# Conditioning sums by column groups, working values in PSUM, SWA scores and one value pair moved: seven edits to a two-block transformer kernel

## What is computed

```python
cond = silu(c)
for i in range(2):
    mod = cond @ ada_w[i] + ada_b[i]               # 1024 -> 6 * 1024
    sh1, sc1, g1, sh2, sc2, g2 = split(mod, 6)
    h = modulate(rms_norm(x, norm_g[i, 0]), sh1, sc1)
    y = nsa_mixer(h, ...) if i == 0 else swa_sink_mixer(h, ...)
    x = x + (1 + g1) * rms_norm(y, norm_g[i, 1])
    h = modulate(rms_norm(x, norm_g[i, 2]), sh2, sc2)
    y = (relu(h @ w_up) ** 2) @ w_down             # 1024 -> 4096 -> 1024
    x = x + (1 + g2) * rms_norm(y, norm_g[i, 3])
```

## Time and profile before

| what | us |
|---|---|
| device time, median of 3 runs (their range) | 2114.76 (2109.31 to 2120.08) |
| profiled execution, its own time | 2111.6 |
| its span | 2109.8 |
| PE busy | 1987.3 (94%) |
| DVE busy | 1208.1 (57%) |
| POOL busy | 950.7 (45%) |
| ACT busy | 699.0 (33%) |

### The profile page before, as it was taken

The page is one execution under the profiler, slowest core; times in us unless marked ns, Lnnn a source line. Parts: engine busy times, 40 slices in busy tenths (PEclk is TensorE's granted clock), DMA queues, the critical chain, the costliest instruction groups (busy, mean ns, idle before and its releaser), DMA issues.

```text
span 2109.8 us, 26670 instructions
## 1 busy us (share of the span) xinstructions
PE 1987.3 (94%) x10136; PEld 1631.9 (77%) x10136; DVE 1208.1 (57%) x1721; ACT 699.0 (33%) x1217; POOL 950.7 (45%) x552
## 2 busy tenths in 40 slices
PE   6999999889999998888999999899999989999997
PEld 5887777668888886766788888787897678888885
DVE  7576776873745667656623426686463338546163
ACT  3343554321222233553322223342343332222122
POOL 1465554454454445444444444542374134444442
PEclk9999999999999999999999999998999999999998
DMA  7774322435555424622222323221243123323221
GB/s 280 230 215 162 110 91 90 150 140 180 195 173 190 170 71 130 180 81 70 90 91 99 100 90 100 71 79 62 100 140 100 40 70 100 98 91 100 92 99 60
DMA packets 79985, 252.16 MB, mean 120 GB/s; under 512 B 12160, under 2 KB 12672, under 8 KB 79616
## 3 DMA queue, kind: packets, MB, share of 16 engines
q1 hardware_dynamic: 79872, 250.61, 35.9%
HBM read 235.21 MB, written 15.37 MB: 119 GB/s over the span
## 4 chain that ended last, share of the span: by engine, by line
PE 69%; issue 12%; DVE 8%; POOL 8%; ACT 3%; POOLq 0%; DVEq 0%; ACTq 0%
PE ps L885 19%; PE ps L887 18%; PE ps L886 18%; POOL wl L785 5%; PE ps L1128 3%; PE ps L1100 2%; PE ps L1071 2%; DVE rs L1933 2%; DVE st L1785 1%; PE ps L1365 1%; PE ps L1026 1%; POOL pr L806 1%; PE ps L1388 1%; ACT pr L2457 1%; POOL al L835 1%
## 5 line engine op out<-in xcount | busy, mean ns | idle before, releaser
L785 POOL TENSOR_TENSOR wl<-raw,wh 128x1024 fp32r<-128x1024 f32 x309 | 777.7, 2522 | 1001.7 <-ACT wh L2313 1001.7
L2313 ACT CAST wh<-raw 128x1024 fp32r<-128x1024 f32 x309 | 322.3, 1049 | 916.7 <-PE ps L887 838.4
L885 PE MATMUL ps<-ah,wh 128*128 128x512 f32 x1240 | 488.4, 394 | 1.4 <-DVE pair L1715 1.4
L886 PE MATMUL ps<-ah,wl 128*128 128x512 f32 x1240 | 483.2, 390 | 0.0
L887 PE MATMUL ps<-al,wh 128*128 128x512 f32 x1240 | 483.1, 390 | 0.0
L885 PE MATMUL ps<-hh,wh 128*128 128x512 f32 x688 | 272.2, 396 | 14.6 <-DVE hl L1935 10.8
L885 PEld LDWEIGHTS ps<-ah,wh 128*128 128x128 f32 x1240 | 233.3, 188 | 52.8 <-issue 3.2
L887 PE MATMUL ps<-hl,wh 128*128 128x512 f32 x688 | 272.4, 396 | 0.0
L886 PEld LDWEIGHTS ps<-ah,wl 128*128 128x128 f32 x1240 | 233.4, 188 | 49.6 <-issue 1.7
L887 PEld LDWEIGHTS ps<-al,wh 128*128 128x128 f32 x1240 | 233.1, 188 | 48.9
L886 PE MATMUL ps<-hh,wl 128*128 128x512 f32 x688 | 270.5, 393 | 0.0
(11 more groups left out here) (360 smaller groups left out, 2915.0 us busy)
## 6 DMA issues: line engine op xcount, KB each, us to landing
raw<-in_units SPq DMA_DIRECT2D x309, 512.0 KB, 3.5
ada_mlp<-in_ada SPq DMA_DIRECT2D x64, 512.0 KB, 3.3
ada<-in_ada SPq DMA_DIRECT2D x16, 512.0 KB, 16.1
qs<-qscr SPq DMA_DIRECT2D x32, 256.0 KB, 3.4
ada_in<-in_ada SPq DMA_DIRECT2D x16, 512.0 KB, 3.5
ks<-kscr SPq DMA_DIRECT2D x24, 256.0 KB, 4.5
x<-in_xT SPq DMA_DIRECT2D x1, 2048.0 KB, 13.4
qscr<-rot_h SPq DMA_DIRECT2D x16, 128.0 KB, 2.4
```

Source lines behind the costliest of these rows:

```text
L785: nc.gpsimd.tensor_tensor(wl[:, slot], raw[:, slot], wh[:, slot].bitcast(F32), ALU.subtract).then_inc(lo_done, 1)
L885: nc.tensor.matmul(out_ap, wh[:, slot, k], high[:, k0 + k], start=first and k == 0, stop=False)
L886: nc.tensor.matmul(out_ap, wl[:, slot, k], high[:, k0 + k], start=False, stop=False)
L2313: a.copy(wh[:, slot], raw[:, slot]).then_inc(hi_done, 1)
```

## The change

1. The conditioning sums of `ada_late` take ones (128 by 32) as the stationary side and the 128 by 1024 sum as the moving side, 128 columns at a time, and write four groups of 32 partitions; DVE copies the row out (`ada_fold`) and TensorE turns it with two transposes (`ada_turn`). The sites are now: in `nsa_out` the sum after the fifth unit and the turn after the seventh; in `mlp0` the sum after the third unit of a block and the turn after the sixth; the last one after the sixth unit of block 7, with its turn in `swa_in`.
2. In NSA, blocks 2 and 0, which lie side by side in a bank, share one mask product of 256 columns.
3. In the setup the conditioning sums in the making, the scale coefficient's input and the scaled chunks of the first norm are in PSUM.
4. In the MLP the square is made as max(b, 0) times `rs` and written to PSUM bank 5 or 7; ACT and the subtraction read it there.
5. In SWA the first two works' scores, maxima, exponentials and scaling are placed inside `swa_in` (`EARLY`), TensorE's after the eighth of its eleven units; they use banks 4 to 7. The two batches of `turn` change places, with a count of `p_scaled` for each. The last query rotary is no longer split.
6. Two of the value units of the memory are multiplied in the fourth head of the cross-attention (`last_values`), in two halves, where the other heads have query units.
7. Some DVE steps change places (`ada_take(7)` behind a rotary), and a ScalarE copy of the setup is ahead of the root.

```diff
-TURNS = {"nsa": (((0, 0),), ((1, 0), (3, 384)), ((2, 0),)), "swa": (((0, 0), (1, 256)), ((2, 0), (3, 256)))}
-COPIES = {"nsa": (("act", 512), ("dve", 512), ("dve", 256)), "swa": (("dve", 512), ("act", 384))}
+TURNS = {"nsa": (((0, 0),), ((1, 0), (3, 384)), ((2, 0),)), "swa": (((2, 0), (3, 256)), ((0, 0), (1, 256)))}
+COPIES = {"nsa": (("act", 512), ("dve", 512), ("dve", 256)), "swa": (("act", 384), ("dve", 512))}
...
-        return b if self.nsa else 2 * (w % 2) + b
+        if self.nsa:
+            return b
+        return 2 * (w % 2) + b + (4 if w < EARLY else 0)
...
+                        if i == 2:
+                            op.then_inc(p_scaled, 1)
                 op.then_inc(p_scaled, 1)
 
             def centre(w):
...
-                    for part in range(2):
+                    for part in range(1 if plan.nsa and i == 2 else 2):
                         nc.tensor.matmul(o, qs[:, Q_SLOT[j], i * P:(i + 1) * P], ks[:, slot, part, k0 * P:k1 * P],
-                                         start=part == 0, stop=False)
-                    if plan.nsa or i == 0:
+                                         start=part == 0 and not (plan.nsa and i == 0), stop=False)
+                    if plan.nsa and i == 2:
+                        mm = nc.tensor.matmul(o, qs[:, Q_SLOT[j], i * P:(i + 1) * P], ks[:, slot, 1, k0 * P:k1 * P],
+                                              start=False, stop=False)
+                    elif plan.nsa and i == 0:
+                        mm = nc.tensor.matmul(ps[:, bank, col - P:col + P], ident_r[:],
+                                              mask_r[:, 1:2].to_broadcast([P, 2, P]), start=False, stop=True)
+                    elif plan.nsa or i == 0:
                         mm = nc.tensor.matmul(o[:, width - P:width], ident_r[:], mask_r[:, 1], start=False, stop=True)
                     else:
                         mm = nc.tensor.matmul(o, ident_r[:], mask_r[:].rearrange("p a k -> p (a k)"), start=False, stop=True)
...
                 for b, parts in enumerate(plan.turns):
+                    if not plan.nsa:
+                        pe.wait_ge(p_scaled, 2 * n - plan.nth0 + 1 + b)
...
         def ada_late(k):
             pe.wait_ge(adc_used, 8 * (k + 1))
-            ada(ps[:, 6, 8 * k:8 * k + 8], acc_mlp[:, k % 2])
+            for half in range(2):
+                for j in range(4):
+                    m = 4 * half + j
+                    mm = nc.tensor.matmul(ps[32 * j:32 * j + 32, 6, half * P:(half + 1) * P], small("ones")[:, 0:32],
+                                          acc_mlp[:, k % 2, m * P:(m + 1) * P], start=True, stop=True)
+            mm.then_inc(ada_sum, 1)
+        def ada_turn(k):
+            pe.wait_ge(ada_copied, k + 1)
+            for half in range(2):
+                mm = nc.tensor.transpose(ps[:, 6, (2 + half) * P:(3 + half) * P], ada_row[:, half * P:(half + 1) * P],
+                                         small("ident"))
+            mm.then_inc(ada_sum, 1)
...
+                        gemm(u, 3, ah, al)
+                    if late:
+                        ada_late(b)
+                    gemm(u + 3, 3, ah, al)
+                    if late:
+                        ada_turn(b)
+                    gemm(u + 6, 2, ah, al)
...
         attention(PLAN_NSA)
-        gemm_squared(FIRST["nsa_out"], ah, al, ready=(o_split, 0), midway=lambda: ada_late(0), adds=True)
+        gemm_squared(FIRST["nsa_out"], ah, al, ready=(o_split, 0), adds=True,
+                     between=lambda c: ada_late(0) if c == 4 else ada_turn(0) if c == 6 else None)
         mlp("mlp0", 0)
         gemm_first(FIRST["swa_in"], ah, al, A_READY["swa_in"])
-        gemm(FIRST["swa_in"] + 3, UNITS_SWA_IN - 3, ah, al)
+        gemm(FIRST["swa_in"] + 3, 1, ah, al)
+        ada_turn(7)
+        gemm(FIRST["swa_in"] + 4, 4, ah, al)
+        attention(PLAN_SWA, early=True)
+        gemm(FIRST["swa_in"] + 8, UNITS_SWA_IN - 8, ah, al)
+        assert done[0] % RING == 3
         attention(PLAN_SWA)
...
+        def last_values(i):
+            assert LAST_VALUES % RING == 3
+            n, t = done[0], slice(i * P, (i + 1) * P)
+            if i == 0:
+                pe.wait_ge(lo_done, LAST_VALUES + 2)
+                bank_free(n)
+            o = ps[:, n % RING, i * 256:i * 256 + 256].rearrange("p (a f) -> p a f", a=2)
+            for k in range(DC):
+                nc.tensor.matmul(o, mh[:, k, t], wh[:, 0:4:3, k], start=k == 0, stop=False)
+                nc.tensor.matmul(o, mh[:, k, t], wl[:, 0:4:3, k], start=False, stop=False)
+                mm = nc.tensor.matmul(o, ml[:, k, t], wh[:, 0:4:3, k], start=False, stop=k == DC - 1)
+            if i:
+                mm.then_inc(unit_used, 2)
+                done[0] += 1
         xscores(0, 0)
         for h in range(4):
             if h < 3:
                 gemm(XQ0 + 2 * h + 2, 1, ah, al)
+            else:
+                last_values(0)
             xturn(h, 0)
             xscores(h, 1)
             if h < 3:
                 gemm(XQ0 + 2 * h + 3, 1, ah, al)
+            else:
+                last_values(1)
             xturn(h, 1)
             if h < 3:
...
             def scaled(c):
-                v.scalar_tensor_tensor(out=tt[:, c % 3], in0=src_t[:, c], scalar=gain(c), in1=inv,
...
                 dve.wait_ge(high_made, n0 + c + 1)
-                t, h = tt[:, c % 3], high[:, c].bitcast(F32)
...
 
+        def so_far(i):
+            return ps[:, 2 * i:2 * i + 2].rearrange("p b s -> p (b s)")
         dve.wait_ge(cond_done, 1)
         for k in range(8):
             dve.wait_ge(ada_in[k], 16)
             if k == 0:
-                op = v.tensor_scalar(acc0[:], ada0[:, k], cond[:, 0:1], None, ALU.mult)
+                op = v.tensor_scalar(so_far(0), ada0[:, k], cond[:, 0:1], None, ALU.mult)
             else:
-                op = v.scalar_tensor_tensor(out=acc0[:], in0=ada0[:, k], scalar=cond[:, k:k + 1], in1=acc0[:],
-                                            op0=ALU.mult, op1=ALU.add)
+                op = v.scalar_tensor_tensor(out=acc0[:] if k == 7 else so_far(0), in0=ada0[:, k], scalar=cond[:, k:k + 1],
+                                            in1=so_far(0), op0=ALU.mult, op1=ALU.add)
             op.then_inc(ada_first, 1)
...
                 w = ada0[:, 12 + i]
                 if i == 0:
-                    op = v.tensor_scalar(acc1[:], w, cond[:, 4:5], None, ALU.mult)
+                    op = v.tensor_scalar(so_far(1), w, cond[:, 4:5], None, ALU.mult)
                 else:
-                    op = v.scalar_tensor_tensor(out=acc1[:], in0=w, scalar=cond[:, 4 + i:5 + i], in1=acc1[:],
-                                                op0=ALU.mult, op1=ALU.add)
+                    op = v.scalar_tensor_tensor(out=acc1[:] if i == 3 else so_far(1), in0=w, scalar=cond[:, 4 + i:5 + i],
+                                                in1=so_far(1), op0=ALU.mult, op1=ALU.add)
                 op.then_inc(scale_part_made, 1)
                 dve.wait_ge(scale_part_made, i + 1)
...
-        ada_read_out(1, ps[:, 7, 0:8])
-        ada_coef(0, 0)
-        norm("nsa_in", x, coef_at(0, 0), coef_at(0, 1), ah, al, root=False, after=first_shift)
+        link(v.tensor_tensor(ps[:, 7, 8:16], ps[:, 7, 0:8], small("ada_b")[:, 8:16], ALU.add))
+        link(v.scalar_tensor_tensor(out=coef[:, 0, 0], in0=ps[:, 7, 8:16], scalar=1.0, in1=small("norm_g")[:, 0:8],
+                                    op0=ALU.add, op1=ALU.mult))
+        norm("nsa_in", x, coef_at(0, 0), coef_at(0, 1), ah, al, root=False, after=first_shift, place=first_place)
 
 
...
         def ada_take(k):
 
-            dve.wait_ge(ada_sum, 4 + k)
-            ada_read_out(4 + k, ps[:, 6, 8 * k:8 * k + 8])
+            dve.wait_ge(ada_sum, 2 * k + 5)
+            turned = ps[:, 6, 2 * P:4 * P].rearrange("p (a f) -> p a f", a=2)[:, :, 0:P:32]
+            at0 = 8 * (4 + k)
+            link(v.tensor_tensor(mod[:, at0:at0 + 8].rearrange("p (a f) -> p a f", a=2), turned,
+                                 small("ada_b")[:, at0:at0 + 8].rearrange("p (a f) -> p a f", a=2), ALU.add))
+        def ada_fold(k):
+            dve.wait_ge(ada_sum, 2 * k + 4)
+            v.tensor_copy(ada_row, ps[:, 6, 0:2 * P]).then_inc(ada_copied, 1)
 
         def mlp(layer):
...
                     k = hid[0]
-                    t = rs[:, k % 2]
-                    v.tensor_scalar(t, bank(), 0.0, None, ALU.max).then_inc(evac, 1)
-                    dve.wait_ge(evac, banks[0])
-                    v.tensor_tensor(t, t, t, ALU.mult).then_inc(hid_sq, 1)
+                    b, t = bank(), ps[:, 5 + 2 * (k % 2)]
+                    link(v.tensor_scalar(rs[:, k % 2], b, 0.0, None, ALU.max))
+                    if c >= 2:
+                        dve.wait_ge(hid_made, k - 1)
+                    v.scalar_tensor_tensor(out=t, in0=b, scalar=0.0, in1=rs[:, k % 2], op0=ALU.max,
+                                           op1=ALU.mult).then_inc(evac, 1)
```

(11 more changed lines are left out.)

143 lines of the change are left out of this document (87 added, 56 removed).

## The result

The changed kernel took 2087.57 us (median of 4 runs, 2085.17 to 2093.22), the kernel before 2112.03 (4 runs beside it): ratio 0.9886, 95% interval 0.9853 to 0.9919. A second series of five gave 2087.69 and 0.9883 (0.9865 to 0.9900). The forecast was 2087. That the two agree within 0.6 us is in part luck: from the execution that the sum started from, 2111.6, the terms took off 26.7 and 2.1 was added for the level of the runs, while the measured difference is 24.5; and some terms came out otherwise and cancel.

A forecast was written before the change was run, and what follows sets the result against it. TensorE, busy 94% of the span, was taken as the bound. Terms summed to -27.6, or -26.7 with 0.9 for the clock: 2111.6 to 2084.9, given as 2087 for the level of runs; range 2075 to 2101 (8 in 10).

The forecast's parts named there:

- first sum in `nsa_out`, with the clock: In `nsa_out`, the conditioning sum moved two units forward makes TensorE wait about 2.1 us: 1.3 us more, plus 0.9 for clock.
- `mlp0`, waits: In `mlp0`, two TensorE waits for the low part (7.9 us) and the low clock behind them (3.0) go: 10.9 less.
- `mlp0`, seven sites: In `mlp0`, each of seven conditioning sites falls from 1.70 to 0.9 us: 5.6 us less in all.
- cross-attention: Before `xo`, value products moved from `kv` cover waits and keep the clock up: 6.8 us less.
- so I save about 0.05 each: NSA mask: two products of 128 columns become one of 256 in each of 32 works, 1.6 us less.
- eight are 0.25: At a conditioning site, eight column-group products take 0.25 us, from a norm row read as 16 products in 0.62.
- the rival with 0.4 for each way: Conditioning sites: entering and leaving the tiled mode drains some 0.4 us each, so eight sites gain nothing; 2093 us, 10 in 100.
- So it keeps its 1.28: In `mlp0`, DVE's conditioning step with two SBUF inputs starts ahead of POOL's operation and stays at 1.28 us.
- The rival's mechanism: In the MLP, the conditioning step falls behind POOL's subtraction, a chunk costs 6 us, both waits stay; 2101 us, 10 in 100.
- I see the same 880.3 to 880.6 for it: In SWA, scores of works 4 and on still start then, set by queries stored after the last rotary.
- about 6 us: In SWA, TensorE does its work earlier, then stands in one piece for about 6 us; clock loss 1.5 to 2.
- The rival of the late queries: SWA hand-over: late query loads hold early scores and units behind; 4 to 10 us late 15 in 100, slower than before 2.

The follow-up runs named there:

- the run with half of the edit: Kernel before with the MLP square reading PSUM but written to SBUF, where ScalarE and the subtraction read it: 2100.7 us, ratio 0.9948 (0.9935 to 0.9962).

## Why the prediction was right, and where its terms were not

The terms, in the order of the sum:

| term | forecast | shown by the stages |
|---|---|---|
| setup | -2.1 | -2.3 |
| NSA mask | -1.6 | none in the mean (alone -1.1 to +3.8 by its ratio) |
| first sum in `nsa_out`, with the clock | +1.3 + 0.9 | +2.2 (+1.3 or +2.9) |
| `mlp0`, waits | -10.9 | -11.9 |
| `mlp0`, seven sites | -5.6 | -5.8 |
| `mlp1` | -2.9 | -3.2 |
| SWA | +1.0 | -0.5 (means of 5 and 7 profiles) |
| cross-attention | -6.8 | -7.5 |
| feed-forward network | none | +2.1 |

- **Setup.** The mechanism was as stated, and so was the copy that still stands behind GpSimd (1.78 us).
- **NSA mask.** This step failed: "so I save about 0.05 each", 1.6 us in 32 works. It holds in the four executions with 10.2 us at the lower clock (172.3 to 172.5 us against 174.0), and in the six others the stage is as long as before or longer, up to 178.3. I counted products and gave this stage no term for the clock. Nor did I ask what ends a work: ScalarE's exponentials ended eleven of TensorE's waits before (6.2 and 5.2 us), twelve with the edit (8.3 and 5.5), so part of the freed time became waits. That these waits bring the lower clock is possible, but not shown.
- **First sum.** The wait of 2.1 us came as 1.98. Of the seven profiles that have it, four have 3.4 us at the lower clock behind it (stage 48.7) and three don't (47.1): 2.2 in the mean.
- **Conditioning sites.** 1.0 for my 0.9, against an old 1.8 for my 1.7; the difference was right, but by luck. The step "eight are 0.25" came out as 0.58 up to the next unit's product. The row that it was taken from, x16 of `L963`, is eight products with two records each, not sixteen products (the x16 of `L1026` and `L1191` are eight products too), so it gives 0.45 for eight. The turn with its ways in and out cost 0.23 where I had 0.45, and entering and leaving the column groups about 0.1 each (0.32 and 0.34 where two products start 0.23 apart), the 0.1 that I had estimated. So the rival with 0.4 for each way falls.
- **MLP.** The waits, the clock behind them and the square's 0.70 us were as worked out; `mlp0` gained 1 us more than these, which I haven't traced. In the period of 5.4 us before, the subtraction stood with 0.69; its mean in `mlp0` was 1815 ns, so it was held too, but that cost TensorE only 0.4 us (the run with half of the edit). "So it keeps its 1.28" was wrong for the conditioning step: the mean rose by 0.33 us. The rival's mechanism was there, its size was not.
- **SWA.** "I see the same 880.3 to 880.6 for it" held within 0.2 us in the first profile, counted from the first unit of `swa_in`; in the five others with early scores that wait there, the fifth work starts 77.7 to 79.4 us after that unit, against 78.9. The stand of "about 6 us" in one piece came as 1.76 us for DVE's `vv` and 2.80 for the queries, with small ones beside them; no row that I read had the first. The batches' new order costs a little (1.49 against 1.36 five times), where I gave nothing. Whether the early scores gain or lose is below what these runs tell. The rival of the late queries was there with 0.41 to 1.15 us in six of the seven profiles with early scores and with nothing in the seventh, far from the 27 at which the whole gain would be gone.
- **Cross-attention.** The mechanism was right: the clock stayed up (1.00 for 12.06 us); mis-sized by 0.7.
- **Feed-forward network.** A cost of 2.1 us in a stage that no edit touches; none of my rivals had it.

Mask and feed-forward network are 3.7 us to the bad, the other terms together 4 to the good. The terms shown add up to -26.9; by their ratios the two series of the changed kernel gave -24.1 and -24.7, with intervals of -17 to -31 and -21 to -29. Which execution of before and of after one takes moves this sum by several microseconds of clock.

## What to carry to other kernels

Where DVE and GpSimd work side by side, look first for the DVE operation with two SBUF inputs that stands ahead of TensorE's need, and give it one input from PSUM; here freeing the others shortened the stages by another 0.7 us. Before products are taken out of a stage, read who ends TensorE's waits there and how the stage's length goes with the clock over several executions: here 1.6 us of products gave nothing in the mean. A float32 product can leave two records, so count a row's records against the loop that issues them. And before a step is moved forward, find the row in which its input is made.

## What was not expected of the hardware

**An edit tipped a race far behind it.** In the feed-forward network, which no edit touches, the stretch from the first `hh` product to the end takes 293.0 to 293.5 us in the three programs without the MLP edit, and 295.3 to 297.5 in the eleven with it. The timelines part at one copy. Before, and then with the MLP edit alone:

```profile
1774.37 0.43 DVE L2269 CAST hh<-uc 128x512 f32 x1
1774.44 2.60 POOL L785 TENSOR_TENSOR wl<-raw,wh 128x1024 fp32r<-128x1024 f32 x1 [0.77 <-ACT wh L2313]
```

```profile
1756.86 2.39 POOL L784 TENSOR_TENSOR wl<-raw,wh 128x1024 fp32r<-128x1024 f32 x1 [0.61 <-ACT wh L2314]
1756.94 2.60 DVE L2270 CAST hh<-uc 128x512 f32 x1
```

When the copy starts 0.07 us ahead of GpSimd's subtraction it takes 0.43 us; when it starts 0.08 us behind, 2.60, and the copies behind it start 0.2 to 3.7 us later than in the programs without the edit; TensorE then waits 2.46 us for a low part, one unit into the stretch, instead of 0.79, with 3.4 us at the lower clock after it. In all fourteen profiles it went by the program, not by the execution (0.07 or 0.08 us ahead in three, 0.07 to 0.10 behind in eleven); why the MLP edit shifts the two starts by 0.15 us against each other stays open.

**Copies contend too.** That copy has one SBUF input and was held 2.2 us, and the setup's shift copy 1.6 (1.78 against 0.17 of the small operation ahead of it). The Trainium skill (SBUF — State Buffer, Who interferes with whom) excepts the two-port modes from its rule for one SBUF input, which the prediction cites without this exception, and says that copies can enter them. The traces agree in that both copies were held; which mode they ran in, none of them shows.

**The same program, another clock.** Two executions of the changed kernel had 13.7 and 23.9 us at the lower clock in the NSA attention, for 3.3 us of time; the whole spans differ by 6.9. A stage's gain of 1 or 2 us needs the lengths of several profiles.
